# Gathering an expert layer's first pair from centred rows, with the norm's weight and bias put on the gathered tokens

## What is computed

```python
for i in range(2):
    m = even_mixer(x, ...) if i % 2 == 0 else odd_mixer(x, ...)
    x = layer_norm(DN_ALPHA * x + m, ln1_g[i], ln1_b[i])
    f = hier_moe(x, ...)
    x = layer_norm(DN_ALPHA * x + f, ln2_g[i], ln2_b[i])

def layer_norm(x, g, b):
    return (x - mean(x)) * rsqrt(var(x) + eps) * g + b

def hier_moe(x, w_rg, b_rg, w_re, b_re, w1, w3, w2):
    group = argmax(softmax(x @ w_rg + b_rg))                # 4 groups
    top_v, top_i = top_k(the group's 8 of x @ w_re + b_re, 2)
    gate = softmax(top_v) * g_prob[group]
    y = sum over both: (silu(x @ w1[e]) * (x @ w3[e])) @ w2[e] * gate
```

## Time and profile before

| | before |
|---|---|
| time, median of 3 executions | 1518.52 us (1516.85 to 1519.75) |
| the profiled execution, its own time | 1515.62 us |
| its span, first to last instruction | 1513.3 us |
| mean granted TensorE clock | 0.997 of full speed |
| busy: PE / DVE / ACT / POOL | 97% / 37% / 31% / 10% of the span |
| expert stretch of layer 0 / layer 1 | about 144 to 588 us / 734 to 1180 us |
| read from memory | 500.40 MB |

### The profile page before, as it was taken

How to read it: one execution, slowest core, us unless ns; L and a number is a source line. 1 busy time by engine, 2 the same in 40 slices (tenths; PEclk the granted TensorE clock), 3 DMA queues, 4 the chain that set the end, 5 groups by cost and what they waited for, 6 DMA issues and landing times.

```text
span 1513.3 us, 19291 instructions
## 1 busy us (share of the span) xinstructions
PE 1463.3 (97%) x7758; PEld 884.6 (58%) x7758; DVE 566.1 (37%) x1169; ACT 475.7 (31%) x837; POOL 154.9 (10%) x126
## 2 busy tenths in 40 slices
PE   8989999999999999999999999999989999999998
PEld 6756454544544444977544545445434686888886
DVE  5675111111111113037321111211111489699975
ACT  4551111111111113456111111111111562577654
POOL 0211000000000002952100000000000620001200
PEclk9999999999999999999999999999999999999999
DMA  8655999999999999735899999999999855554410
GB/s 301 246 227 223 405 422 427 428 428 426 428 428 427 426 424 400 289 147 237 329 411 425 429 427 428 427 427 427 428 427 409 320 200 202 188 211 180 168 55 28
DMA packets 76229, 502.70 MB, mean 332 GB/s; under 512 B 4720, under 2 KB 6000, under 8 KB 49136
## 3 DMA queue, kind: packets, MB, share of 16 engines
q1 hardware_dynamic: 75280, 495.18, 80.3%
q0 software_dynamic: 864, 6.29, 1.0%
HBM read 500.40 MB, written 1.05 MB: 331 GB/s over the span
## 4 chain that ended last, share of the span: by engine, by line
PE 83%; DVE 7%; DMA 5%; ACT 2%; issue 2%; SPq 1%; POOL 0%; DVEq 0%; ACTq 0%
PE bank L1110 26%; PE bank L1143 14%; PE bank L969 9%; PE bank L1056 7%; DMA ring<-in_w_up 4%; PE bank L1426 3%; PE bank L1070 3%; PE bank L1454 3%; DVE w_low L2494 2%; PE bank L878 2%; PE bank L1428 2%; PE bank L1003 2%; PE bank L897 1%; PE bank L816 1%; DVE arena L2518 1%
## 5 line engine op out<-in xcount | busy, mean ns | idle before, releaser
L1110 PE MATMUL bank<-ring,arena 128*64 128x512 f32 x1280 | 283.6, 598 | 12.9 <-issue 10.1
L1110 PEld LDWEIGHTS bank<-ring,arena 128*64 128x64 f32 x1280 | 94.2, 138 | 197.3 <-issue 195.8
L1110 PE MATMUL bank<-arena 128*64 128x512 f32 x576 | 168.3, 592 | 2.4 <-issue 2.4
L2113 DVE TENSOR_TENSOR arena<-arena,bank 128x512 f32<-128x512 f32 x32 | 22.0, 687 | 382.3 <-PE bank L1110 382.3
L1143 PE MATMUL bank<-ring,arena 128*64 128x512 f32 x640 | 141.7, 595 | 2.4 <-ACT arena L1608 2.4
L1426 PE MATMUL bank<-x_split,w_high 128*128 128x512 f32 (+1 forms) x408 | 136.3, 385 | 0.2 <-DVE x_split L1921 0.2
L1056 PEld LDWEIGHTS bank<-SEL,x_by_row 128*128 128x128 f32 x1024 | 116.7, 192 | 25.8 <-issue 24.3
L2127 DVE SCALAR_TENSOR_TENSOR y_low<-bank,ST,y_high 128x512 fp32r<-128x512 f32 x64 | 48.0, 751 | 202.4 <-ACT y_high L1612 202.4
L1056 PE MATMUL bank<-SEL,x_by_row 128*128 128x128 f32 x1024 | 122.8, 278 | 0.0
L1612 ACT ACTIVATE y_high<-bank,ST 128x512 fp32r<-128x512 f32 x64 | 44.0, 687 | 245.6 <-PE bank L1143 245.6
L1110 PEld LDWEIGHTS bank<-arena 128*64 128x64 f32 x576 | 55.4, 137 | 109.7 <-issue 109.7
(11 more groups left out here) (370 smaller groups left out, 2285.2 us busy)
## 6 DMA issues: line engine op xcount, KB each, us to landing
ring<-in_w_gate SPq DMA_DIRECT2D x32, 2048.0 KB, 27.6
ring<-in_w_up SPq DMA_DIRECT2D x32, 2048.0 KB, 22.9
ring<-in_w_down SPq DMA_DIRECT2D x32, 2048.0 KB, 24.7
arena<-in_w_gate SPq DMA_DIRECT2D x18, 2048.0 KB, 24.5
arena<-in_w_up SPq DMA_DIRECT2D x18, 2048.0 KB, 24.4
arena<-in_w_down SPq DMA_DIRECT2D x18, 2048.0 KB, 26.4
ring<-in_ffn_up SPq DMA_DIRECT2D x12, 2048.0 KB, 7.9
ring<-in_w_in SPq DMA_DIRECT2D x8, 2048.0 KB, 14.0
```

What stands on the lines that cost most here:

```text
L1110: last = nc.tensor.matmul(bank[4 + m][64 * e:64 * e + 64, :], XG[:, c, 64 * e:64 * e + 64], w[e][:, c, :], start=(c == 0), stop=(c == C - 1))
```

## The change

Layer norm is linear once mean and variance are known, so the change applies its pieces at other places. The router multiplies raw rows: WR is first multiplied by the weight (`sum_routes`), a matmul with ones sums its columns (`add_route_sums`) so that the mean can be taken out of WR and the bias put on the logits (`fold_routes`), and the row's 1/std is applied to 36 logits. Each tile's choice is made on its own (`choose`). The first gather reads Z = (x - mean) / std, which ACT writes, and weight and bias, brought into columns by one-column transposes (`norm_columns` in layer 0, `row_columns` in both), are put on the gathered tokens. The normed X, its copy XP (now by ACT) and the four residual matmuls come later: the residuals stand between the up matmuls of pair 0 and the gather for pair 1.

```diff
 # SP: the tenth block, n = 9
-                        sp.wait_ge(logits_done, l + 1)
+                        sp.wait_ge(logits_done, T * (l + 1))
...
 # POOL
-            rows_of_x(0)
             next_norm_rows(0, 1)
...
 # PE
             def experts(s, n, g, matrix, x_rows, first=False, last_of=None, next_pair=True, up_free=None,
-                        first_rows=None, columns_ready=None):
+                        first_rows=None, columns_ready=None, before_gather=None):
...
                     last.then_inc(done, 1)
+                if before_gather is not None:
+                    before_gather()
                 if next_pair:
...
+            def norm_columns():
+                pe.wait_ge(ln_loaded, 16)
+                for a in range(2):
+                    for c in range(C):
+                        last = nc.tensor.transpose(bank[0][:, a * C + c:a * C + c + 1], LNR[0:1, a, c * P:(c + 1) * P],
+                                                   ident[0:1, 0:1])
                 last.then_inc(rank_done, 1)
+            def row_columns():
+                for a in range(2):
+                    for c in range(C):
+                        last = nc.tensor.transpose(bank[6][:, a * C + c:a * C + c + 1],
+                                                   LNR[0:1, a, :].rearrange("p (q c) -> p c q", c=C)[:, c, :], ident[0:1, 0:1])
+                last.then_inc(rank_done, 1)
+            def route(l, name, g0):
+                logits(l, name, 1, [0])
+                keep_clock(7, 1)
+                x_transposes(name, g0, 1, [1])
+                logits(l, name, 1, [1])
+                row_columns()
+                keep_clock(7, 2)
+                pe.wait_ge(r_one, T * l + 1)
+                nc.tensor.matmul(bank[4][:, 256:256 + EXPERTS], earlier, ELOG[:, 0, :], start=True, stop=True)
+                nc.tensor.matmul(bank[4][:, 320:320 + EXPERTS], ones, ELOG[:, 0, :], start=True, stop=False)
+                keep_clock(7, 1)
+                pe.wait_ge(r_one, T * l + 2)
+                nc.tensor.matmul(bank[4][:, 320:320 + EXPERTS], earlier, ELOG[:, 1, :], start=False, stop=True)\
+                    .then_inc(rank_done, 1)
+            def moe_layer(l):
                 pe.wait_ge(moe["sel_ready"], PAIRS * l + 1)
-                pe.wait_ge(xp_ready, T * (l + 1))
-                gather(moe, x_by_row)
+                pe.wait_ge(z_ready, 3 * l + 3)
+                gather(moe, z_by_row)
...
+                def finished_rows():
+                    pe.wait_ge(x_ready, 4 * l + 2)
+                    for t in range(T):
+                        keep_residual(t)
+                    pe.wait_ge(xp_ready, 2 * l + 2)
...
+            def beside_even(t, n, c):
+                if (t, n, c) == (0, 1, 0):
+                    add_route_sums(0)
+                if (t, n, c) == (1, 0, 1):
+                    x_transposes("ln0", G_EO, 0)
+                if (t, n, c) == (1, 1, 0):
+                    pe.wait_ge(route_weights, 2)
+                    logits(0, "ln0", 0)
+                if (t, n, c) == (1, 1, 2):
+                    x_transposes("ln0", G_EO, 1, [0])
+            project_differential(beside_even)
...
             for n in range(1, 5):
                 split_project_t(S_QKV, n)
+            add_route_sums(1)
...
 # ACT
+                act.wait_ge(z_ready, 3 * l + 3)
+                for c in range(4):
+                    last = nc.scalar.activation(XG[:, c, :], bank[6][:, c * P:(c + 1) * P], ACT.Identity,
+                                                scale=row_gain[:, c:c + 1], bias=row_shift[:, c:c + 1])
...
+                act.wait_ge(x_ready, 4 * l + 2)
+                for t in range(T):
+                    nc.scalar.copy(XP[:, t, :, :], X[:, t, :].rearrange("p (q c) -> p c q", c=C)).then_inc(xp_ready, 1)
...
 # DVE
             def mixed_norm(l, g0, name):
                 for t in range(T):
                     for n in range(2):
+                        if (t, n) == (1, 1):
+                            choose(l, 0)
                         add_half(g0, t, n, ALPHA)
                         last = half_stats(t, n, X[:, t, 512 * n:512 * n + 512])
                     link(last)
                     norm_variance(t)
-                    dve.wait_ge(ln_loaded, 16 * (2 * l + 1))
-                    link(v.scalar_tensor_tensor(X[:, t, :], X[:, t, :], mv[:, t, 0:1], LNR[:, 0, :], ALU.subtract,
-                                                ALU.mult))
-                    norm_scale(t)
-                evac_token(name, T - 1)
+                    inverse_root(var_l[:, t:t + 1], rs_l[:, t:t + 1])
+                    v.scalar_tensor_tensor(neg_mean[:, t:t + 1], mv[:, t, 0:1], -1.0, rs_l[:, t:t + 1], ALU.mult, ALU.mult)\
+                        .then_inc(x_prepared, 1)
+                choose(l, 1)
...
+            sum_routes(0)
             for g, copied in enumerate((tr_act, tr_dve)):
...
+            fold_routes(0)
+            mixed_norm(0, G_EO, "ln0")
```

More of the change, by code:

```diff
@@ L868, in recurrence_tile, with project_out @@
                 return LX[:, c, t * P:(t + 1) * P]
-            def project_out(g0, i, rows=range(C), tile=mixed_tile, beside=None, first=0, final=C - 1):
+            def project_out(g0, i, rows=range(C), tile=mixed_tile, beside=None, first=0, final=C - 1, between=None):
                 for t in range(T):
@@ L879, in project_out @@
                                                     slot(i[n], C, 512)[:, c, :], start=(c == first), stop=(c == final))
+                            if between is not None and c != final:
+                                between(t, n, c)
                         if rows[-1] == final:
@@ new lines, in x_transposes @@
+            def x_transposes(name, g0, t, halves=range(2)):
+                for h in halves:
+                    k = TR[name][0] + 2 * t + h
+                    pe.wait_ge(pj_free[t], g0 + h + 1)
+                    pe.wait_ge(tr_dve if k % 2 else tr_act, (k - 4) // 2 + 1)
+                    for j in range(4):
+                        c = 4 * h + j
+                        last = nc.tensor.transpose(bank[4 + k % 4][:, j * P:(j + 1) * P], X[:, t, c * P:(c + 1) * P], ident)
+                    last.then_inc(tr_done, 1)
@@ new lines, in logits @@
+            def logits(l, name, t, halves=range(2)):
+                for h in halves:
+                    pe.wait_ge((tr_act, tr_dve)[h], TR[name][0] // 2 + t + 1)
+                    for c in range(4 * h, 4 * h + 4):
+                        last = nc.tensor.matmul(bank[4 + t][:, 0:ROUTE], x_tile(c, t), WR[:, l, c, :],
+                                                start=(c == 0), stop=(c == C - 1))
+                    if h:
+                        last.then_inc(logits_done, 1)
+            def norm_columns():
+                pe.wait_ge(ln_loaded, 16)
+                for a in range(2):
+                    for c in range(C):
+                        last = nc.tensor.transpose(bank[0][:, a * C + c:a * C + c + 1], LNR[0:1, a, c * P:(c + 1) * P],
+                                                   ident[0:1, 0:1])
+                last.then_inc(rank_done, 1)
@@ new lines, in row_columns, with add_route_sums @@
+            def row_columns():
[4 more added lines that the diff above has]
+                last.then_inc(rank_done, 1)
+            def add_route_sums(l):
+                pe.wait_ge(route_weights, 2 * l + 1)
+                nc.tensor.matmul(bank[5][:, 0:2 * ROUTE], ones, ROUTE_SUMS[:, :, :].rearrange("p a r -> p (a r)"),
+                                 start=True, stop=True).then_inc(rank_done, 1)
@@ new lines, in keep_residual @@
+            def keep_residual(t, halves=range(2)):
+                for half in halves:
+                    nc.tensor.matmul(bank[2 * t + half][:, :], residual, X[:, t, 512 * half:512 * half + 512],
+                                     start=True, stop=False, skip_group_check=True)
+            def route(l, name, g0):
[12 more added lines that the diff above has]
+                    .then_inc(rank_done, 1)
@@ new lines, in moe_layer @@
+                dve.wait_ge(moe["gather_hi"], PAIRS * l + 1)
+                dve.wait_ge(z_ready, 3 * l + 3)
+                for c in range(4, C):
+                    last = v.tensor_scalar(XG[:, c, :], bank[7][:, (c - 4) * P:(c - 3) * P], row_gain[:, c:c + 1],
+                                           row_shift[:, c:c + 1], ALU.mult, ALU.add)
+                last.then_inc(moe["xg_hi"], 1)
+                dve.wait_ge(top_done, l + 1)
+                link(v.tensor_reduce(rtop2[0:1, :], bank[5][0:1, 0:P], AX, ALU.max))
```

241 lines of the change are left out of this document (133 added, 108 removed).

## The result

The changed kernel takes 1524.13 us (median of 6 executions, 1522.21 to 1526.67), the kernel before 1517.42 us beside it (6 executions, 1513.76 to 1519.75). The ratio is 1.0045, with a 95% interval from 1.0029 to 1.0061: slower by 6.7 us. It is within the range of the prediction (1516.0 to 1524.5), near its upper end, but it isn't the "no change" of the forecast. The profiled execution takes 1522.33 us, its span is 1520.5, against 1515.62 and 1513.3.

A forecast was written before the change was run, and what follows sets the result against it. DMAs bound the expert stretch, so a layer ends a constant after pair 1's down: 3.5 - 3.0 + 0.65 = 1.1 us later in layer 0, 0.9 in layer 1; 1518.52 + 2.0 = 1520.5 us, range 1516.0 to 1524.5.

The forecast's parts named there:

- Rival B: At each layer's end: it follows the first gate, not pair 1's down; 4.9 us less, 1513.6; chance 0.13.
- The walk through the route: From projection to first gather, priced by instruction: gather 3.0 us earlier in layer 0, 2.8 in layer 1.
- the 0.65 of `norm_columns`: Sixteen one-column transposes on PE between 79.7 and 80.91, partly inside a wait: 0.65 us excess delays everything behind.
- rival A: Route's one-column transposes read with an eight-element step, slowing weight loads: 1.3 to 1.9 us per layer, 1523.1 to 1524.3; chance 0.25.
- Step 1: Layer 0's route up to the gather's start: 141.3 instead of 144.24, 3.0 us earlier.
- step 2: Behind the first gate: four residual matmuls enter between up and gather, adding 3.5 us before pair 1's down.
- cheap transposes: One-column transposes at 0.06 us each: 0.9 less per route, 0.65 less for `norm_columns`, -0.5 in all, 1518.0.
- missed terms: Allowance in the range for terms the sum left out: 2 us on either side.
- The dips: DMA rates while the queue runs dry before the plateau: near zero for 2 us around 170 and 182.

## Why the prediction was right, and where it was wrong

**What bounds: right.** A layer ends a constant time behind pair 1's down. From the issue behind it to layer 1's first mixer load it is 374.8 us in the kernel before, 375.2 in the change, 376.1 and 375.9 with the residuals late and with the columns by DMA; in layer 1 (to the issue at 1167.79, 1173.73) 376.3 and 376.2. Over all fourteen profiles the layer 0 distance is 374.7 to 376.9 (the longest with the residuals in pair 2), while pair 1's down itself lies between 197.5 and 208.9: it is a constant to within two microseconds. Rival B, the lead of the first gate counts, is out: with the residuals late the first gather of layer 0 started 1.6 later than in the change, and yet pair 1's down came 1.9 and the layer's end 0.9 earlier (577.53 for 578.47).

**The walk through the route: right, but for the clock.** Logits at 134.9 (135.1 predicted), the one-column transposes 1.84 (1.87), the choices end at 131.6 and 138.4 (131.9, 138.7), a filler stands before the last rank matmul, the residuals cost 3.54 (3.5). ACT's passes for Z take 2.3 each, the dear end of what was allowed, and end at 136.8 in time. Without the slow clock the route is 0.2 worse in layer 0 and 0.5 in layer 1 where 0.45 (1.1 less the 0.65 of `norm_columns`) and 0.7 were predicted.

**Mis-sized: `norm_columns`.** Predicted 0.65 on the path, measured nothing. PE's timeline of the change:

```profile
78.55 1.12 PE L1355 MATMUL bank<-arena 128*128 128x128 f32 x8
79.60 1.14 PE L1208 MATMUL bank<-KT,LNR 1*128 1x1 f32 x16
80.75 0.66 PE L1344 MATMUL bank<-KT,prob_over_mixed 128*128 128x128 f32 x4
```

Sixteen take 1.15, 0.072 each, and the next row starts no later than before (80.75 for 80.91), where the wait of 1.08 stood. The transposes with a step of eight elements take 0.115. So rival A's mechanism seems to be there, a factor of 1.6, only on a base that was lower than assumed (the two kinds differ in the step and in place and bank, and no run changed the step alone); its price, 1.3 to 1.9 per layer over the forecast, is not. That its total (1523.1 to 1524.3) is the measured one is a coincidence.

**The step that failed** is the sum's silence on the clock. Step 1 prices the two fillers behind the transposes at 1.72 and the transposes at their PE time alone: every row of the kernel before had 1.00 here, and the prediction took 1.00 over, without a reason. Measured are 3.49 and 3.25 for the fillers. The sentence on the residuals in step 2, "where they stood in PE's wait for DVE (removing them gives nothing)", may be a part of it, but no run put the residuals alone back. In the kernel before, PE's route from 127.3 to 144.2 held four residual matmuls and seven fillers of 512 columns, in the change from 130.7 to 142.75 it holds four fillers, and sixteen transposes of one column are added. Over all profiles the routes with a fall of the clock are:

| kernel | routes with a fall |
|---|---|
| before | 0 of 2 |
| before without fillers | 2 of 2 |
| one-column transposes in the route (six kernels, the change twice) | 14 of 14 |
| columns by DMA, waits as they are (two) | 2 of 4 |
| columns by DMA, waits filled (three) | 0 of 6 |

Shown by these runs: with the one-column transposes in the route the clock falls, even with the waits around them filled; without them it falls in some of the routes; without them and with the waits filled it holds; and in the kernel before, whose route has no such transposes, it falls once the fillers are gone. In the rows below a fall costs 1.4 to 2.7, wherever it lands (the one of ten microseconds above costs more): on the fillers (3.49 for 1.80; in the second profile of the change, layer 1, 3.58 and 1.85 for 1.80 and 0.94) or on the gather (5.46 for 3.84). The kernel before has sixteen transposes of 128 columns in its route and no fall, but no run here separates the kind of instruction from its one column.

**Where luck comes in.** The forecast was 2.0 us slower, and the profiled spans differ by 7.2. Of this the clock is 4.5 and the part behind pair 1's down of layer 1 is 1.1; neither is in the sum. The 1.6 left are close to the 1.35 that the sum has without `norm_columns`. So the walk was right, but that 1524.13 lies inside the range is luck: the range was made for cheap transposes, missed terms and rival A, and not for a fall of the clock, and a fall as long as that of layer 1 in the second profile in both layers would have left it.

**The dips were shallower than said.** Rates near zero for 2 us around 170 and 182 were forecast. The lowest windows of the change have 262 GB/s in 172 to 174, 295 in 184 to 186 and 311 in 204 to 206, at 427 GB/s 0.5 to 0.8 us of missing work each. But the windows between them are low as well (299 in 176 to 178): from 170 to 188 us the change lacks 2.8 us of work by this count, the kernel before 0.6. The 2.2 more are what the prediction's "2 or 3 us longer" says, but they are spread and not a standstill, and they come from a gather whose lead was 1.5, not 3.0, and from the residuals ahead of pair 1's loads; the rows don't part the two.

**What stays open.** The clock falls in layer 1's attention in seven profiles (the change twice, residuals late, fillers moved, no fillers, waits filled, residuals in pair 2) and not in five others with the same instructions there (before with and without fillers, columns by DMA, that and the residuals late, the same with the route's waits filled); which it will be can't be told from the rows. With one-column transposes in layer 0's route it fell in six of six profiles, without them in one of six (fillers in the attention left out); what could link the two isn't shown. So it is open whether these 1.4 us belong to the change. And from layer 1's end to the end of the run the change takes 1.2 us more than the kernel before (339.6 against 338.4 from the first load behind it to the store of the output), though no instruction differs there; in the second profile of the change it is 341.3, in the two fastest kernels 338.5 and 338.4, in the kernel before without its fillers 342.5. The granted clock is full there in every profile, so the clock isn't the cause. No run tests it, and differences of a microsecond or two between single profiles can come from there.

## What to carry to other kernels

A matmul whose result nobody reads can be load-bearing: before a wait is emptied or a stretch is thinned, look at the granted clock there and count what wide work is left, and try the kernel with the waits filled. Work that PE must do anyway goes where the DMAs have a backlog, not between the first gate and the point at which the queue fills: 3.5 us of matmuls per layer cost 3.5 us in pair 0, less than a microsecond in pair 4. And small constants that have to change their layout come cheaper by a DMA in the prologue than by transposes on the critical path.

## What the runs showed of the hardware

- The granted clock went to 0.50 (1.2 GHz) behind a stretch in which PE's rows show it busy: but for one wait of 0.67 us it is so from 130.7 to 137 us. Matmuls of one and of 36 columns are 3.8 us of this, four transposes and one filler of 512 columns the rest.
- It also went to 0.50 in stretches of 512-column matmuls, at the end of a wait of PE of 2.1 to 3.1 us or about a microsecond behind it, in the kernel before (waits ahead of 510.88 and 1102.55) as in the change. A wait of 2.66 us at 479 to 481 in the kernel before had no fall behind it.
- One-column transposes take no longer at the low clock: in layer 1 of the run with the fillers moved, eight pass in 0.96 us at a granted clock of 1.00 (from 736.68) and eight in 0.96 at 0.50 (from 739.53). Fillers and gather pay for the fall.
- A weight load of one partition with unit step, with one moving column, passes in 0.072 us; with a step of eight elements in 0.115. The prediction drew on the Trainium skill, "TensorE: Matmul & The Clock Gate", section on LDWEIGHTS, for a load time that goes by the columns and not by the contraction's depth. Both have 128 columns, so here it goes by something else as well. Nor does the depth leave it alone: in PE's weight loads sixteen of one partition with unit step take 1.06 us, 0.066 each, while seven of 128 partitions for the transposes of the kernel before take 0.80, 0.114 each. The measurement decides. The penalty that the Trainium skill, "SBUF — State Buffer", section on the DMA port swizzle, states for an access that crosses into a new 16-byte line is in line with it.
- Two fillers between the transposes moved the fall instead of preventing it, and it lasted longer: from 144 to 150 us in layer 0, some 10 us in layer 1, against 3 in the change's first profile and up to 7 in its second. Waits and the gather stand in these stretches; whether they are the reason wasn't tried.
